# Column sums of a convolution's two norms in a hybrid decoder step: tiles added on VectorE, one product with the ones instead of four

## The reference

```python
q, k, v, a, gate = jnp.split(h @ p["w_in"], ...)
u = a * jax.nn.sigmoid(gate)
c = causal_dwconv(u_ctx, p["conv_w"]) + p["conv_b"]        # width 31
c = jax.nn.silu(layer_norm(c, p["ln_conv_g"], p["ln_conv_b"]))
mix = jnp.concatenate([rms_norm(attn, p["g_out_attn"]), rms_norm(c, p["g_out_conv"])], axis=-1)
```

## Time and profile before

| | |
|---|---|
| median of 3 runs | 1849.55 us (1849.14 to 1853.33) |
| profiled execution, its own time | 1853.08 us |
| its span | 1851.3 us |
| mean granted TensorE clock of it | 0.98 |
| TensorE busy (matmul records) | 1754.1 us, 95% |
| VectorE busy | 1130.6 us, 61% |
| ScalarE busy | 872.6 us, 47% |

### The profile page before, as it was taken

The page is one execution under the profiler, slowest core; times in us unless marked ns, Lnnn a source line. Parts: engine busy times, 40 slices in busy tenths (PEclk is TensorE's granted clock), DMA queues, the critical chain, the costliest instruction groups (busy, mean ns, idle before and its releaser), DMA issues.

```text
span 1851.3 us, 30583 instructions
## 1 busy us (share of the span) xinstructions
PE 1754.1 (95%) x12222; PEld 1625.9 (88%) x12222; DVE 1130.6 (61%) x2075; ACT 872.6 (47%) x1646; POOL 2.2 (0%) x12
## 2 busy tenths in 40 slices
PE   7999999878999799999999899999999999999998
PEld 6999999745656798988877899999999999999998
DVE  5499995365666577743545776664466543576633
ACT  6322222533455566655545555543554543555432
POOL 0000000000000000000000000000000000000000
PEclk9999999998999899999999999999999999999999
DMA  7233222244321454444353344444444544444543
GB/s 230 66 114 111 78 90 97 69 153 155 127 81 41 136 175 126 137 160 124 116 167 107 91 126 118 136 140 137 133 136 142 163 132 137 137 140 143 150 131 102
DMA packets 349219, 233.74 MB, mean 126 GB/s; under 512 B 7979, under 2 KB 322465, under 8 KB 349071
## 3 DMA queue, kind: packets, MB, share of 16 engines
q1 hardware_dynamic: 342907, 220.24, 39.1%
q10 hardware_dynamic: 6172, 11.55, 1.8%
HBM read 220.68 MB, written 11.50 MB: 125 GB/s over the span
## 4 chain that ended last, share of the span: by engine, by line
PE 81%; DVE 9%; ACT 6%; issue 3%; DMA 0%; ACTq 0%; DVEq 0%
PE bank L1177 76%; PE bank L1174 6%; ACT whi L590 1%; DVE wlo L1742 1%; DVE op_lo L1729 1%; ACT Pp L807 1%; DVE Y L1729 1%; DVE KTS L1921 1%; ACT wide L604 1%; DVE Sx L2038 1%; DVE XT L2050 1%; DVE op_x L2053 1%; DVE cv L1729 1%; DVE Pp L1733 0%; DVE STD L1865 0%
## 5 line engine op out<-in xcount | busy, mean ns | idle before, releaser
L1177 PE MATMUL bank<-op_hi,whi 128*128 128x352 f32 x1632 | 541.6, 332 | 14.1 <-DVE op_lo L1729 9.0
L1177 PE MATMUL bank<-op_hi,wlo 128*128 128x352 f32 x1632 | 527.4, 323 | 0.0
L1177 PE MATMUL bank<-op_lo,whi 128*128 128x352 f32 x1632 | 527.0, 323 | 0.0
L1742 DVE TENSOR_TENSOR wlo<-raw,whi 128x1024 fp32r<-128x1024 f32 (+1 forms) x312 | 373.8, 1200 | 243.3 <-ACT whi L590 243.0
L590 ACT ACTIVATE whi<-raw 128x1024 fp32r<-128x1024 f32 (+1 forms) x312 | 325.2, 1043 | 292.0 <-PE bank L1177 89.2
L1177 PEld LDWEIGHTS bank<-op_hi,whi 128*128 128x128 f32 x1632 | 309.4, 190 | 23.7 <-issue 19.5
L1177 PEld LDWEIGHTS bank<-op_lo,whi 128*128 128x128 f32 x1632 | 310.3, 190 | 0.5
L1177 PEld LDWEIGHTS bank<-op_hi,wlo 128*128 128x128 f32 x1632 | 309.4, 190 | 0.0
L1177 PE MATMUL bank<-fhi,whi 128*128 128x352 f32 x528 | 171.2, 324 | 0.0
L1177 PE MATMUL bank<-fhi,wlo 128*128 128x352 f32 x528 | 170.7, 323 | 0.0
L1177 PE MATMUL bank<-h1hi,whi 128*128 128x352 f32 x480 | 159.4, 332 | 3.0 <-DVE h1lo L1729 3.0
(11 more groups left out here) (271 smaller groups left out, 2361.0 us busy)
## 6 DMA issues: line engine op xcount, KB each, us to landing
raw<-in_w_up_dram SPq DMA_DIRECT2D x132, 512.0 KB, 3.8
raw<-in_w_down_dram SPq DMA_DIRECT2D x48, 512.0 KB, 3.8
raw<-in_w_out_dram SPq DMA_DIRECT2D x24, 512.0 KB, 3.8
raw<-in_w_xq_dram SPq DMA_DIRECT2D x24, 512.0 KB, 3.8
raw<-in_w_xo_dram SPq DMA_DIRECT2D x24, 512.0 KB, 3.8
raw<-in_w_in_dram SPq DMA_DIRECT2D x20, 512.0 KB, 3.9
raw<-in_w_down_dram SPq DMA_DIRECT2D x24, 384.0 KB, 3.3
cached<-in_cache_win_k_dram SPq DMA_DIRECT2D x8, 1024.0 KB, 6.0
```

The source lines that it names most:

```text
L1177: return pe.matmul(out, lhsT, rhs, start=first, stop=last, skip_group_check=shared)
L1742: dve.tensor_tensor(wlo[v % SLOTS][:, 0:nk, :], raw[v % SLOTS][:, 0:nk, :], whi[v % SLOTS][:, 0:nk, :].bitcast(F32), ALU.subtract).then_in ...
```

## The change

VectorE adds the four tiles of a sum first and TensorE makes one product with the ones of the result.

- The means: `conv_mean_sum(j)` adds the four tiles of `C` one after the other into a new tile `CSUM[j % 2]`, three dependent additions. `CSUM` lies where the convolution's input `U` was, so VectorE first waits for the transposes that read `U` (`cst_t`). `conv_mean` is one product.
- The squares: ScalarE writes the four squares to `SQ[1]`, `SQ[2]`, `SQ[3]`, `SQ[0]`; `conv_square_sum` adds SQ[1] + SQ[2], SQ[3] + SQ[0] and the two results, into `SQ[0]`. `conv_square_mean` is one product of `SQ[0]`. ScalarE waits for the previous sum before it writes the first three squares of the next, and for its product before the fourth.
- The places: in `CONV_AT` the third mean moves from behind third (17, 2) to behind (17, 1); the third chunk's first square sum from (18, 1) to (18, 2); the last square sum (second, third chunk) from (19, 2) into the attention stage, behind the first two scores of step 0. ScalarE's root of it moves to the start of that stage.

```diff
-    CONV_AT = {(17, 0): (("mean", 0),), (17, 1): (("mean", 1),), (17, 2): (("square", 0, 0), ("mean", 2)), (18, 0): (("square", 0, 1),),
-               (18, 1): (("square", 0, 2),), (19, 0): (("square", 1, 0),), (19, 1): (("square", 1, 1),), (19, 2): (("square", 1, 2),)}
+    CONV_AT = {(17, 0): (("mean", 0),), (17, 1): (("mean", 1), ("mean", 2)), (17, 2): (("square", 0, 0),), (18, 0): (("square", 0, 1),),
+               (18, 2): (("square", 0, 2),), (19, 0): (("square", 1, 0),), (19, 1): (("square", 1, 1),), ("step", 0): (("square", 1, 2),)}
...
         def conv_squares(second, j):
             c = CONV_ORDER[j]
+            m = second * CH + j
             for k in range(CT):
-                n = (second * CH + j) * CT + k
                 act.wait_ge(*at("cs" if second else "cc", (c, k)))
-                if n >= 4:
-                    act.wait_ge(*at("csq_used", n - 4))
-                act.activation(SQ[n % 4][:, :], C[:, k, c * CW:(c + 1) * CW], ACT.Square).then_inc(*mark("csq", n))
+                if m:
+                    act.wait_ge(*(at("csum", m - 1) if k < CT - 1 else at("csq_used", m - 1)))
+                act.activation(SQ[(k + 1) % CT][:, :], C[:, k, c * CW:(c + 1) * CW], ACT.Square).then_inc(*mark("csq", (m, k)))
...
             if (n_in, c) == (19, 2):
-                for j in range(CH):
-                    conv_root(1, j)
+                conv_root(1, 0)
+                conv_root(1, 1)
...
+        conv_root(1, CH - 1)
         for s in range(LAST_STEP + 1):
             sample(*sample_slot(s, 0))
...
         def conv_mean(j):
             c, b = CONV_ORDER[j], CONV_BANK["mean", j]
-            pe.wait_ge(*at("conv", "end"))
             take(b, "cc", (c, CT - 1))
-            for k in range(CT):
-                ins = mm(bank[b][:, 0:CW], ones_c[:, :], C[:, k, c * CW:(c + 1) * CW], k == 0, k == CT - 1)
-            ins.then_inc(*mark("cmean", c))
+            pe.wait_ge(*at("csum", ("mean", j, CT - 1)))
+            mm(bank[b][:, 0:CW], ones_c[:, :], CSUM[j % 2][:, :], True, True).then_inc(*mark("cmean", c))
 
         def conv_square_mean(second, j):
-            b = CONV_BANK["square", second, j]
-            take(b, "csd", second * CH + j)
-            for k in range(CT):
-                n = (second * CH + j) * CT + k
-                pe.wait_ge(*at("csq", n))
-                mm(bank[b][:, 0:CW], ones_c[:, :], SQ[n % 4][:, :], k == 0, k == CT - 1).then_inc(*mark("csq_used", n))
+            b, m = CONV_BANK["square", second, j], second * CH + j
+            take(b, "csd", m)
+            pe.wait_ge(*at("csum", m))
+            mm(bank[b][:, 0:CW], ones_c[:, :], SQ[0][:, :], True, True).then_inc(*mark("csq_used", m))
...
             if s < NP:
                 scores(s, 0)
+            if s == 0:
+                conv_square_mean(1, CH - 1)
...
+        def conv_mean_sum(j):
+            c = CONV_ORDER[j]
+            part = [C[:, k, c * CW:(c + 1) * CW] for k in range(CT)]
+            if j >= 2:
+                dve.wait_ge(*at("cmean", CONV_ORDER[j - 2]))
+            for k in range(1, CT):
+                if k > 1:
+                    dve.wait_ge(*at("csum", ("mean", j, k - 1)))
+                dve.tensor_tensor(CSUM[j % 2][:, :], CSUM[j % 2][:, :] if k > 1 else part[0], part[k], ALU.add).then_inc(*mark("csum", ("mean", j, k)))
+
+        def conv_square_sum(second, j):
+            m = second * CH + j
+            dve.wait_ge(*at("csq", (m, 1)))
+            dve.tensor_tensor(SQ[1][:, :], SQ[1][:, :], SQ[2][:, :], ALU.add).then_inc(*mark("csum", (m, "a")))
+            dve.wait_ge(*at("csq", (m, 3)))
+            dve.tensor_tensor(SQ[3][:, :], SQ[3][:, :], SQ[0][:, :], ALU.add).then_inc(*mark("csum", (m, "b")))
+            dve.wait_ge(*at("csum", (m, "b")))
+            dve.tensor_tensor(SQ[0][:, :], SQ[1][:, :], SQ[3][:, :], ALU.add).then_inc(*mark("csum", m))
+
         conv(len(jobs))
+        dve.wait_ge(*at("conv", "end"))
+        dve.wait_ge(*at("cst_t", 0))
+        conv_mean_sum(0)
+        conv_mean_sum(1)
         conv_centre(0)
+        conv_mean_sum(2)
         conv_centre(1)
+        conv_square_sum(0, 0)
+        conv_centre(2)
+        conv_square_sum(0, 1)
         conv_scale(0, 0)
-        conv_centre(2)
+        conv_square_sum(0, 2)
         conv_scale(0, 1)
+        conv_square_sum(1, 0)
         conv_scale(0, 2)
+        conv_square_sum(1, 1)
+        conv_square_sum(1, 2)
```

More of the change, by code:

```diff
@@ L100 @@
           "fst_t": "cst_t", "prm_t": "cst_t", "mt": "h1t", "att_t": "h1t", "mhi": "h1hi", "mlo": "h1lo", "asd": "xsd",
-          "ass": "xss", "csd": "std", "crs": "rstd", "mkv": "zt", "cmean": "csq_used", "att8": "att",
+          "ass": "xss", "csd": "std", "crs": "rstd", "mkv": "zt", "cmean": "csq_used", "csum": "cc", "att8": "att",
           "mexp": "sexp", "mpn": "spn", "mpt": "spt", "mptr": "sptr", "mpv": "spv", "msc": "ssc", "ktm": "ktsa", "cv0": "aev", "w_lo_a": "w_lo", "qzw": "qz", "cached2": "ident"}
@@ L236, in layout @@
     SQ = [mn(f"SQ{i}", 129024 + 1408 * i, [P, CW]) for i in range(4)]
+    CSUM = [mn(f"CSUM{i}", 125440 + 1408 * i, [P, CW]) for i in range(2)]
     SQA = [mn(f"SQA{i}", 134656 + 1408 * i, [P, CW]) for i in range(4)]
@@ L408, in y_free @@
         if (name, c) == ("out", 0):
-            eng.wait_ge(*at("csq_used", 2 * CH * CT - 1))
+            eng.wait_ge(*at("csq_used", 2 * CH - 1))
             eng.wait_ge(*at("asq_used", CH * AT - 1))
@@ L488, in _ @@
         window(1)
-        sp.wait_ge(*at("csq_used", 2 * CH * CT - 1))
+        sp.wait_ge(*at("csq_used", 2 * CH - 1))
         sp.wait_ge(*at("cn", (CONV_ORDER[CH - 1], CT - 1)))
@@ L662, in conv_squares @@
             c = CONV_ORDER[j]
+            m = second * CH + j
             for k in range(CT):
-                n = (second * CH + j) * CT + k
                 act.wait_ge(*at("cs" if second else "cc", (c, k)))
-                if n >= 4:
-                    act.wait_ge(*at("csq_used", n - 4))
-                act.activation(SQ[n % 4][:, :], C[:, k, c * CW:(c + 1) * CW], ACT.Square).then_inc(*mark("csq", n))
+                if m:
+                    act.wait_ge(*(at("csum", m - 1) if k < CT - 1 else at("csq_used", m - 1)))
+                act.activation(SQ[(k + 1) % CT][:, :], C[:, k, c * CW:(c + 1) * CW], ACT.Square).then_inc(*mark("csq", (m, k)))
         def conv_root(second, j):
             n = second * CH + j
-            act.wait_ge(*at("csq_used", n * CT + CT - 1))
+            act.wait_ge(*at("csq_used", n))
             if not second and n >= 2:
```

## The result

The changed kernel takes **1838.52 us** (median of 4 runs, 1836.54 to 1839.63); the kernel before, run beside it, takes 1849.35 (1847.49 to 1853.33). The ratio is **0.9937, 95% interval 0.9919 to 0.9956**: faster by more than the 0.3% that can be told from nothing. The forecast was 1834.0 with a range of 1830 to 1841. The sign and the range held; the gain is 10.8 us where 15.6 were forecast.

The account below looks back on a forecast made before the run. TensorE was taken to bound the stretch, with a few waits. Walking three engines through trace durations gave 16.0 − 7.4 + 6.2 + 1.8 = 16.6 us, less 1.0 for clock, 15.6: median 1849.55 becomes 1834.0, range 1830 to 1841.

Parts of the forecast that it names:

- The products: Convolution stage, TensorE: nine sums of four products become nine single ones, 16.0 us less, all on the chain.
- The means without a wait: Three mean sums on VectorE are ready before TensorE asks at 307.0 and 311.5: no wait.
- Waits ahead of the square sums: TensorE waits 0.95, 3.29, 1.14, 2.02 us at sums 0, 3, 4, 5, none at 1, 2: 7.40 against 6.22.
- VectorE hidden: 27 additions, 14 us of VectorE work, where two of its idle gaps alone hold 27 us.
- The rest shifts stiffly: Everything behind the convolution stage shifts stiffly, first key transposes about 16 us earlier.
- The clock: Convolution stage: the low clock's 1.80 us at the last sum is gone; 1.0 us is lost after the waits.
- The median by the same subtraction: The 15.6 us, summed against the profiled 1853.08, is also taken off the median 1849.55: 1834.0.
- rival A: The clock falls after each of the four waits, costing 7.2 us instead of 1.0: 1840.2 us; chance 0.10.
- B: VectorE is late at all six square sums, 19.7 us of waits: 1845.3 us; chance 0.04.
- C: The gain is absorbed in the attention stage, its first window loads relatively no earlier: about 1848 us; chance 0.03.
- D: Slower: lower clock from 380 to 460 adds 23 us on the chain: 1856 us; chance 0.03.
- my marks for being wrong: Waits over 12 us; clock at 0.5 over some 7 us between 303 and 352; or key-transpose lead gone at end.

Follow-up runs that it names:

- the means alone: The kernel before with only the three means summed on VectorE, squares and order as before: 1846.85 us, ratio 0.9975.
- series 3: Repeat of the change on another chip, beside the kernel before and kernels with needless products: the change took 1836.84 us, ratio 0.9923.
- series 1: Repeat of the change on one chip, beside the kernel before and kernels with parts of the change: the change took 1839.96 us, ratio 0.9950.
- later: The change with square sums 3 and 4 moved one projection third later, against the kernel before: 1838.04 us, ratio 0.9934.
- filled kernel: The change or "later" with needless products with the ones put into TensorE's waits ahead of square sums: ratios to before from 0.9880 to 0.9945.

## Why the prediction held, and where it was off

- **The products**, 16.0 us: right. Nine sums in 18 records, 0.75 alone where eight records took 2.53; the means alone price at 5.6 against 5.3. (The row of six records at 313.29 in the earlier trace rows ends where its view ended; the sum has eight, in 2.53 us. The price rests on the starts of rows and is not touched.)
- **The means without a wait**: right, TensorE asks at 307.1 and 311.5 and does not stop.
- **Waits ahead of the square sums**: right to 0.02 us at sums 0, 3 and 5 of the profiled run (1.26, 3.25 and 2.00 in series 3's), and none at 1 and 2. The 1.14 at sum 4 did not show in the profiled run because the low clock stood in its place; in series 3's profile of the change the wait is 0.91. In the other kernels the wait ahead of sum 0 came out up to 0.6 us longer than the walk has it (1.55 for 0.95, 2.07 for 1.5).
- **VectorE hidden**: right in kind, with 12.6 us more work for it instead of 14 and no addition slower than 0.53. The additions on the chain are the two behind the last square, as the 1.0 us of the walk has it.
- **The rest shifts stiffly**: right but for the clock's 1.8 us between the first and the last key copy.
- **The clock: this is the term that was mis-sized.** I put down the 1.80 us of the earlier trace rows as gone and 1.0 as added: +0.8 for the change. Measured against before, at the fitted price, the clock cost 0.0042 × 1200 = 5.0 us in series 1 and 0.0008 × 1200 = 1.0 in series 3. The credit came from a single execution, and the low clock behind the last square sum is common to both kernels (six of nine open waits), so a median cannot be credited with its absence. Of the cost only a part lies where I looked for it. The first profile of the change has 13 us at the lower level in the stage and stands 4.1 us behind series 3's at VectorE's first running sum of the norm (613.2 and 609.1); the other two have none in the stage. That is 1.4 us in the mean of the three, near the 1.0. What series 1's profile lost, 3.4 us, it lost from 1045 to 1300 us, where the prediction has everything shifted stiffly. Why the clock of the change was lower than before's by 0.0042 in that series is open: chance from run to run, or something that the shift does to later stages. With the walk's 14.8 and these prices the change should come out 9.8 and 13.8 us ahead; its medians in these two series are 9.3 and 15.8 ahead, and in the first measurement 10.8.
- **The median by the same subtraction**: the profiled execution of before was 3.5 us above its median at a clock of 0.982, where its 49 later runs have 0.984 on average. By the slope such a distance is 3 us of clock, and the low stretch behind the credit of 1.80 is likely a part of it. The credit belongs to the profiled execution; in the median it was counted on top of a number that is already lower.

That the range held owes something to luck: it was drawn so wide at its upper end to take in rival A, and the median lies nearer to A than to the forecast.

Of the rivals, A (1840.2, the clock falls after every wait) is 1.7 us from the median where the forecast is 4.5 away. As a rule it is too strong: the profiles of the change in series 1 and 3 have the four waits and no low clock in the stage, and the one in series 1 lost its time elsewhere. The Trainium skill, page "TensorE: Matmul & The Clock Gate", section "HAM oscillation — how this bites in real kernels", tells of a kernel in which a wait of some 3 to 5 us for a load, between bursts of products, brought the low clock back each time. Here the trace agrees in part: behind the waits of that length, 3.25 to 3.60 us ahead of square sum 3, the clock fell in three of the five profiles in which they stand open, and behind the shorter last waits of 2.0 to 2.6 us in six of nine. B (VectorE late everywhere) falls: sums 1 and 2 had slack even behind a scaling. C (gain absorbed in attention) falls with the lead of 13.1 at the last key copy. D (slower) falls: the granted clock from 380 to 460 is 0.87, what it was.

Of my marks for being wrong the one on the clock was just reached in the first profile, not passed: about 7 us at the lower level between 303 and 352 (336 to 348, by stretches of 4 us), and as much again right behind, from 352 to 364. It marked the right term.

## What to carry to other kernels

A walk of three engines by the durations of the trace gave each wait to 0.6 us or better where the clock was high, most of them to 0.3, and each part of the change to 0.6; it can be trusted for the order of work. What it leaves out is the granted clock: price it from many runs (here 1.2 us for each 0.001), not from one profiled execution, and do not credit a low stretch of that execution as removed by the edit. When an edit takes work off TensorE but leaves waits of 2 to 3 us ahead of dense work, try needless products in the last of them: here all five such comparisons had a mean clock above before's, and no filled kernel had a slower median than its unfilled fellow where both ran in one series.

## What had not been expected of the hardware

- The mean granted clock goes with most of the spread from run to run of one kernel: within groups the two correlate at −0.91 (0.83 of the variance), and six runs of one kernel went from 1834.19 us at 0.985 to 1844.91 at 0.976.
- Low clock behind a wait of a given length comes in some executions and not in others, with the same instructions ahead: the changed kernel's last wait of 2.00 us was followed by a mean of 0.59 over 8 us in one profile and of 1.00 in two.
- A stretch at the lower clock far from the edit (7 us, between 1100 and 1150) told two profiles of the very same kernel apart by 3.4 us.
- Fewer waits did not mean a higher clock: "later" has one wait less than the change and the lowest clock of all, 0.979. Why is open. Its one long wait, 2.62 us, was followed by 8 us at 0.50 in its profile, which yet has a mean of 0.984; its slower runs, down to 0.974, have no profile. Whether the missing pause of 3.3 us earlier matters was not tried.
